# Attention keys and queries: the rounded-weight products on 512 columns, the bank's halves added on VectorE

## What is computed

```
def shared_kv(h, g, w_kv, w_f, b_f):
    hn = rms_norm_2(h, g)
    kv = (hn @ w_kv).reshape(Bn, S, 2, N_HEADS, HEAD_DIM)
    k = kv[:, :, 0].transpose(0, 2, 1, 3)
    log_f = jax.nn.log_sigmoid((hn @ w_f + b_f).astype(jnp.float32))
    c = jnp.cumsum(log_f, axis=1).transpose(0, 2, 1)
...
def forgetting_attention(xq, w_q, w_o, k, v, c):
    q = (xq @ w_q).reshape(Bn, S, N_HEADS, HEAD_DIM).transpose(0, 2, 1, 3) * (HEAD_DIM ** -0.5)
    logits = jnp.einsum('bhqd,bhkd->bhqk', q, k) + c_q - c_k, causal mask, softmax, times v
```

## Time and profile before

| | |
|---|---|
| median of 3 runs | 1554.76 us (1553.53 to 1554.89) |
| the profiled execution | 1554.81 us |
| its span, first to last instruction | 1553.0 us |
| TensorE busy | 97% of the span |
| VectorE busy | 77% |
| ScalarE busy | 51% |
| mean granted TensorE clock | 0.997 of full speed |
| keys, pieces 2 to 7 | about 1038.9 to 1056.4 us of the span |
| queries and attention | about 1281.7 to 1346 us |

### The profile page before, as it was taken

The page is one execution under the profiler, slowest core; times in us unless marked ns, Lnnn a source line. Parts: engine busy times, 40 slices in busy tenths (PEclk is TensorE's granted clock), DMA queues, the critical chain, the costliest instruction groups (busy, mean ns, idle before and its releaser), DMA issues.

```text
span 1553.0 us, 23704 instructions
## 1 busy us (share of the span) xinstructions
PE 1503.0 (97%) x8186; PEld 1281.3 (83%) x8186; DVE 1203.0 (77%) x2164; ACT 789.9 (51%) x1193; POOL 43.5 (3%) x68
## 2 busy tenths in 40 slices
PE   7989999999999899999999999999999999999997
PEld 6767789888888788887878888888888889888886
DVE  4876477988888888778588878785888886597876
ACT  6547554444434544446796444465544466554443
POOL 4100000000000300000000000000000000000000
PEclk9999999999999999999999999999999999999999
DMA  9635445755555666655244766644766643366661
GB/s 257 186 92 185 136 136 209 264 192 181 193 187 160 172 209 196 189 174 175 66 123 139 227 179 198 189 138 152 209 197 189 189 139 107 106 184 191 195 187 57
DMA packets 258538, 266.16 MB, mean 171 GB/s; under 512 B 10512, under 2 KB 210496, under 8 KB 258224
## 3 DMA queue, kind: packets, MB, share of 16 engines
q1 hardware_dynamic: 255040, 255.87, 54.1%
q0 software_dynamic: 3440, 9.54, 2.1%
HBM read 264.21 MB, written 1.09 MB: 171 GB/s over the span
## 4 chain that ended last, share of the span: by engine, by line
PE 85%; DVE 10%; ACT 3%; issue 2%; DMA 0%; DVEq 0%; SPq 0%; ACTq 0%
PE ps L733 25%; PE ps L649 13%; PE ps L650 13%; PE ps L651 13%; PE ps L735 11%; DVE w_lo L1955 2%; PE ps L732 2%; PE ps L1209 1%; DVE xT_both L1999 1%; PE ps L1352 1%; PE ps L675 1%; ACT w_hi L1455 1%; DVE xn L2164 1%; PE ps L659 0%; ACT xT_both L1464 0%
## 5 line engine op out<-in xcount | busy, mean ns | idle before, releaser
L733 PE MATMUL ps<-xT_both,w_hi 128*128 128x512 f32 x1392 | 492.3, 398 | 1.3 <-DVE w_lo L1960 1.3
L1518 ACT ACTIVATE w_hi<-raw 128x1024 fp32r<-128x1024 f32 x294 | 308.3, 1057 | 159.1 <-PE ps L651 137.0
L1960 DVE TENSOR_TENSOR w_lo<-raw,w_hi 128x1024 fp32r<-128x1024 f32 x294 | 350.5, 1220 | 1.6 <-ACT w_hi L1518 0.2
L735 PE MATMUL ps<-xT_both,w_lo 128*128 128x256 f32 x1218 | 342.1, 281 | 0.0
L733 PEld LDWEIGHTS ps<-xT_both,w_hi 128*128 128x128 f32 x1392 | 256.1, 188 | 52.0 <-DVE w_lo L1960 1.8
L1955 DVE TENSOR_TENSOR w_lo<-raw,w_hi 128x1024 fp32r<-128x1024 f32 (+4 forms) x191 | 225.6, 1211 | 37.7 <-ACT w_hi L1455 35.8
L735 PEld LDWEIGHTS ps<-xT_both,w_lo 128*128 128x128 f32 x1218 | 230.3, 189 | 6.7
L1513 ACT ACTIVATE hid_sil<-hid_sil 128x256 f32<-128x256 f32 x120 | 50.1, 418 | 360.6 <-DVE hid_sil L2025 320.7
L1455 ACT ACTIVATE w_hi<-raw 128x1024 fp32r<-128x1024 f32 (+4 forms) x191 | 193.0, 1048 | 29.6 <-PE ps L651 25.8
L649 PE MATMUL ps<-w_hi,hid_hi 128*128 128x512 f32 x480 | 188.8, 393 | 4.2 <-DVE hid_lo L2072 4.1
L650 PE MATMUL ps<-w_lo,hid_hi 128*128 128x512 f32 x480 | 187.1, 390 | 0.0
(11 more groups left out here) (393 smaller groups left out, 2181.5 us busy)
## 6 DMA issues: line engine op xcount, KB each, us to landing
raw<-in_ffn_w_gate_dram SPq DMA_DIRECT2D x88, 512.0 KB, 4.2
raw<-in_ffn_w_up_dram SPq DMA_DIRECT2D x88, 512.0 KB, 5.3
raw<-in_ffn_w_down_dram SPq DMA_DIRECT2D x88, 512.0 KB, 4.2
raw<-in_w_in_dram SPq DMA_DIRECT2D x40, 512.0 KB, 4.9
raw<-in_w_gate_dram SPq DMA_DIRECT2D x32, 512.0 KB, 3.5
raw<-in_w_up_dram SPq DMA_DIRECT2D x32, 512.0 KB, 4.1
raw<-in_w_down_dram SPq DMA_DIRECT2D x32, 512.0 KB, 3.5
raw<-in_rg_w_in_dram SPq DMA_DIRECT2D x16, 512.0 KB, 4.6
```

The costliest lines, as they stand in the source:

```text
L733: m = pe.matmul(o, hi[:, k, :], both[:, :, k, :], start=k == 0, stop=k == KT - 1)
L735: pe.matmul(ps[:, bank, 0:T], lo[:, k, :], both[:, 0, k, :], start=False, stop=False)
L1518: act.activation(w_hi[:, s, :], raw[:, s, :], ACT.Copy).then_inc(hi_done, 1)
L1960: dve.tensor_tensor(w_lo[:, s, :], raw[:, s, :], w_hi[:, s, :].bitcast(F32), ALU.subtract)\
```

## The change

`channel_major` is replaced by `channel_major_wide` for key pieces 2 to 7, and `q_half` is written in the same form: four (then three) matmuls of 512 columns, four of 256, and in the second half a last one of 512. Pieces 0 and 1 stay as they are. In the eviction of pieces 2 to 7 VectorE first adds the two halves of the bank into `kq_sum`, a 256-column tile in SBUF, waits for this to be written, and multiplies from there.

```
-                channel_major((b + j) % RING, ps[:, j % 4, 0:T], 1)
+                channel_major_wide((b + j) % RING, j % 4, 1, xT_both)
...
+                o = ps[:, j % 4, :].rearrange("p (a t) -> p a t", a=2)
+                for k in range(4 * half, 4 * half + 4 - half):
+                    pe.matmul(o, hi[:, k, :], xT_both[:, :, k, :], start=k == 0, stop=False)
                 for k in range(4 * half, 4 * half + 4):
-                    m = mm3(ps[:, j % 4, 0:T], hi[:, k, :], lo[:, k, :], xT_hi[:, k, :], xT_lo[:, k, :],
-                            k == 0, k == KT - 1)
+                    m = pe.matmul(ps[:, j % 4, 0:T], lo[:, k, :], xT_both[:, 0, k, :], start=False, stop=False)
+                if half:
+                    m = pe.matmul(o, hi[:, KT - 1, :], xT_both[:, :, KT - 1, :], start=False, stop=True)
...
+            kq_sum = hid_sil[:, 0, :]
+            def halves_sum(j, at):
+                if j < 2:
+                    return ps[:, j, 0:T]
+                dve.wait_ge(kq_evicted, at + j)
+                link(dve.tensor_reduce(kq_sum, ps[:, j % 4, :].rearrange("p (a t) -> p t a", a=2), AX_X, ALU.add))
+                return kq_sum
...
                 lo(b + 4 + j)
                 dve.wait_ge(used, b + j + 1)
+                src = halves_sum(j, 0)
...
-                    m = dve.tensor_tensor(fk[0:64, 2 * j + e, :], ps[r, j % 4, 0:T], rb[r, :], ALU.mult)
+                    m = dve.tensor_tensor(fk[0:64, 2 * j + e, :], src[r, :], rb[r, :], ALU.mult)
...
                 dve.wait_ge(used, b + j + 1)
+                src = halves_sum(j, 8)
...
-                    m = dve.scalar_tensor_tensor(fq[0:64, 2 * j + e, :], ps[r, j % 4, 0:T], 0.125, rb[r, :],
+                    m = dve.scalar_tensor_tensor(fq[0:64, 2 * j + e, :], src[r, :], 0.125, rb[r, :],
```

## The result

The changed kernel takes 1562.09 us, median of 5 runs (1560.58 to 1563.71), against 1554.76 before. The ratio is 1.0051, with a 95% interval from 1.0036 to 1.0065: slower by 0.5%, where 1561.5 us was forecast. The profiled execution took 1561.93 us with a span of 1560.1, 7.1 us more than before.

The account below looks back on a forecast made before the run. TensorE was taken to bound the kernel, with VectorE almost without room in the key stage. From 1554.81 us, +3.6 (key stage), +1.6 (clock) and +1.5 (query stage) gave 1561.5 us, range 1558.0 to 1564.0.

Parts of the forecast that it names:

- The bound: Whole kernel: TensorE, busy 97%, sets stage times; in the key stage VectorE has only 0.74 us of room over six pieces.
- The key term, +3.6: Key stage: six added VectorE reductions delay the last eviction, so TensorE waits longer at the forget gate, +3.6 us.
- The clock, +1.6: Forget gate: TensorE's longer pause halves its clock, slowing about 8 of the gate's matmuls, +1.6 us.
- my upper bound of 2.2: Forget gate: the most the clock drop could cost, with all 24 gate matmuls at half speed, 2.2 us.
- The query term, +1.5: Query stage: reductions delay TensorE at four places by 2.1 us, less 0.6 us saved on TensorE, +1.5 us.
- The second drop: First `o_half`: the pause grows to about 1.8 us and the clock drops, adding 1.6 us, 1563.1 us; chance 0.10.
- TensorE's saving: Key and query pieces: the wide form saves TensorE 0.10 us a piece, 0.6 us for each stage's six pieces.
- VectorE keeps up: Last key eviction: VectorE absorbs the reductions, TensorE's saving stands alone and the kernel is not slower, 1553.6 us; chance 0.05.
- no clock drop: Forget gate: the key stage is delayed as forecast but the clock stays up, 1559.9 us; chance 0.12.
- the wide form saves nothing: Key and query matmuls: no TensorE time saved, query stage costs 0.6 us more, key stage the same, 1562.1 us; chance 0.03.

Follow-up runs that it names:

- experiment 7: Kernel before, with VectorE's reduction alone added to six key evictions, reading an SBUF tile, result unused; TensorE as before: 1559.24 us, ratio 1.0033.
- experiment 8: Kernel before, with only key piece 2 in the wide form with its sum: 1554.52 us against 1554.50, ratio 1.0000.
- Experiment 4: Changed kernel with nine filling float32 matmuls ahead of the forget gate's wait: 1560.64 us, against the changed kernel's 1562.09.
- Experiment 6: Changed kernel without VectorE's sums, evicting only the first half of the bank, so one product is left out: 1553.83 us, ratio 0.9996.
- experiment 2: Changed kernel with the keys back in the old form, so only the queries are changed: 1557.52 us against 1554.63, ratio 1.0017.
- experiment 3: Changed kernel with 30 filling float32 matmuls ahead of the forget gate's wait, which delayed the gate: 1567.53 us, ratio 1.0083.
- experiment 10: Changed kernel with the wait for all eight key evictions moved behind the forget gate's matmuls: 1558.17 us, ratio 1.0022.
- experiment 1: Changed kernel with the queries back in the old form, so only the keys are changed: 1559.48 us against 1554.63, ratio 1.0031.

## Why the prediction was right, and where it was not

- **The bound.** VectorE without room in the key stage was the right reading of the earlier trace rows: experiments 7 and 8 show the loss with TensorE untouched, and the 0.74 us of room.
- **The key term, +3.6.** It was +3.0. The sum took 0.72 us to its reader as forecast. Each `lo` behind the first gave 0.11 us back: its successor started 1.15 us after it in place of 1.26, that is 0.08 us before its end. I had excluded this "because `lo` still stands behind a pair of 64-partition evictions". That reason failed: the overlap came although this order stayed. The rows tell the two cases apart by what is read from PSUM. Where VectorE's last read of PSUM ahead of `lo` began at partition 64, as in the second half of an eviction from the bank, and the instruction behind `lo` reads PSUM from partition 0, that instruction came 1.25 us or more after the start of `lo`. So it is in all 108 such places of the fourteen profiles with no wait listed between the two. In the 1918 other places it came after 1.13 to 1.15 us, but for five. In the change only piece 2 is such a place, since the later evictions read SBUF; in experiment 7 none of the six is, since the sum there reads SBUF. No kernel was built to test this.
- **The clock, +1.6.** The mechanism was right and the size too small. It was +2.3 on the gate, and 2.5 with the first value matmuls, just above my upper bound of 2.2. I had counted eight slow matmuls, as behind the earlier pauses. Here the clock was low for all 24, over 6 us with the end of the pause. Experiment 4 measures it at 2.3.
- **The query term, +1.5.** It was +1.35. Experiment 6 has the same matmuls and no sums, and against it the changed kernel starts `fqk(4)` at 11.95 us from the `spread` in place of 11.90, `fqk(5)` at 15.56 in place of 14.94, `fp_transposes(6)` at 27.92 in place of 26.89 and the first `o_half` at 37.66 in place of 35.90. So the sums add 0.05, 0.57, 0.41 and 0.73 us at the four places, where 0.15, 0.63, 0.6 and 0.72 were forecast: 1.76 in place of 2.1, less 0.41 saved in place of 0.6. Only the first place was as good as nothing; the other three waits are there.
- **The second drop.** I gave it 0.10 and left it out of the sum. It was there in the changed kernel's profile and in those of experiments 2 and 4, and absent in those of experiments 3 and 10, each time behind a pause of 1.78 us. It cost 1.65 us in the changed kernel and 1.5 in the other two. As a rival it should have had half of the chance or more.
- **TensorE's saving.** Experiment 6 gives 0.43 and 0.41 us for the two stages, not 0.6 each. That is 0.07 a piece, nearer to the 0.10 read from the trace than to the 0.02 estimated from the formula in the Trainium skill (page "TensorE: Matmul & The Clock Gate", section "Back-to-back issue gap"), and it did not decide anything.
- **The total.** That 1561.5 came within 0.6 us of 1562.09 is in part luck, since errors cancel: 0.6 too much at the gate and 0.15 too much in the queries, 0.85 too little for the clock and 1.65 for the second drop. That makes 1.75 too little for the two stages of the profiled execution, and 1.3 of it was given back in the first block, where that one profile had the cheaper of two falls (0.35 us in place of 1.6).
- **The other rivals.** "VectorE keeps up" and "no clock drop" are refuted for the key stage by the changed profile, "the wide form saves nothing" by experiment 6.

## What to carry to other kernels

When an instruction is added to an engine that is not the busiest, look up its idle time in that stage and not over the span: here VectorE was 77% busy overall and had 0.74 us for six added instructions of 0.72. Then price the pause of the engine that waits twice, as waiting and as clock: of the nine pauses at the gate or the first `o_half` that had grown to 1.78 us or more, seven cost 1.3 to 2.3 us on top of themselves. And look first at whether the wait is in the right place: moving it behind independent work, and an eviction ahead of other work in the queue, gained 2.4 us, more than the 1.2 us that the cheaper arithmetic promised.

## What the runs showed of the hardware

- The clock does not answer to the length of a pause alone. Behind 2.41 to 2.50 us, at the same matmul near 62 us, it fell in eight of the fourteen profiles and not in six. Behind 1.78 us it fell in three profiles (the changed kernel and experiments 2 and 4) and not in two (3 and 10). Behind 2.21, 3.92 and 4.31 us it fell (one, one and two profiles), and behind the 4.17 us in the first block in all fourteen; behind 1.06, 1.49 and 1.56 us it stayed.
- It stayed low for different times: all of the gate's 5.1 us in the changed kernel, less than 4 us in experiment 1 with the same pause of 4.31 us.
- A float32 matmul of 256 columns is listed as two records and takes 0.43 us, as against 0.12 in the rounded format.
- An instruction of VectorE can start 0.08 us before the one ahead of it ends, or 0.03 us behind its end, in the same pair of instructions: from `lo` (1.23 us) to the sum of the halves it took 1.26 us once and 1.15 five times. The later start goes, in 108 of 108 places, with a last read of PSUM from partition 64 and a next one from partition 0.
- Filling matmuls ahead of a wait kept the clock at 1.00 without delaying the end of the wait: nine of them (4.05 us) in front of the gate, where the pause without them was 4.31 us and the clock fell.
